# Sharing out the last layer norm of an encoder layer: GpSimd finishes four token tiles, VectorE takes the moments of four

## The reference: what is computed

```
def layer_norm(x, g, b):
    xf = x.astype(jnp.float32)
    mu = xf.mean(-1, keepdims=True)
    var = jnp.square(xf - mu).mean(-1, keepdims=True)
    return ((xf - mu) * lax.rsqrt(var + LN_EPS) * g + b)

x = layer_norm(DEEPNORM_ALPHA * x + moe(x, ...), ln2_g[l], ln2_b[l])
```

## Time and profile before

| what | value |
| --- | --- |
| three timed executions, median | 1329.71 us |
| the profiled execution's own time | 1325.05 us |
| its span, first to last instruction | 1323.2 us |
| busy: PE, DVE, ACT, POOL | 1235.7, 732.8, 590.0, 196.5 us |
| share of the span: PE, DVE, ACT, POOL | 93%, 55%, 45%, 15% |
| chain that ended last, by engine | PE 72%, DMA 7%, DVE 7%, issue 5% |

### The profile page before, as it was taken

The page is one execution under the profiler, slowest core; times in us unless marked ns, Lnnn a source line. Parts: engine busy times, 40 slices in busy tenths (PEclk is TensorE's granted clock), DMA queues, the critical chain, the costliest instruction groups (busy, mean ns, idle before and its releaser), DMA issues.

```text
span 1323.2 us, 21973 instructions
## 1 busy us (share of the span) xinstructions
PE 1235.7 (93%) x8066; PEld 1112.4 (84%) x8066; DVE 732.8 (55%) x1760; ACT 590.0 (45%) x1428; POOL 196.5 (15%) x244
## 2 busy tenths in 40 slices
PE   7999899999999999997799999998899999999993
PEld 6998788888788888886677888897889999999882
DVE  3110355654555455555768876458455565556358
ACT  3221334443444444444543332222365666566455
POOL 0000001200120021011111121001032333233212
PEclk9999999999999999998799999899999999999997
DMA  6534643373437343673354433514889999999773
GB/s 196 158 119 126 161 112 93 81 185 84 108 82 194 79 107 94 159 182 89 98 192 178 152 114 111 223 64 132 306 264 275 265 280 290 272 265 292 188 269 143
DMA packets 157906, 224.35 MB, mean 170 GB/s; under 512 B 40016, under 2 KB 109392, under 8 KB 157776
## 3 DMA queue, kind: packets, MB, share of 16 engines
q1 hardware_dynamic: 146064, 180.28, 45.8%
q0 software_dynamic: 9216, 33.56, 11.1%
q10 hardware_dynamic: 2544, 9.44, 1.8%
HBM read 141.15 MB, written 52.20 MB: 146 GB/s over the span
## 4 chain that ended last, share of the span: by engine, by line
PE 72%; DMA 7%; DVE 7%; issue 5%; SPq 3%; ACT 3%; POOL 1%; DVEq 1%; ACTq 0%; POOLq 0%
PE bank L800 16%; PE bank L802 16%; PE bank L801 16%; PE bank L907 8%; PE bank L794 5%; PE bank L894 4%; PE bank L883 3%; SPq L534 3%; PE bank L884 2%; DMA d_work<-in_w_up 2%; PE bank L1017 2%; DMA acc_scratch<-d_work,dstc 2%; DMA Q<-stage_lo 1%; DVE w_gu_lo L1782 1%; DVE d_work L1980 1%
## 5 line engine op out<-in xcount | busy, mean ns | idle before, releaser
L1262 ACT ACTIVATE b_work<-b_work 128x256 f32<-128x256 f32 (+3 forms) x288 | 148.1, 514 | 267.9 <-DVE b_work L1598 267.1
L800 PE MATMUL bank<-xgT_hi,w_gu_hi 128*128 128x256 f32 x704 | 202.4, 288 | 5.2 <-DVE xgT_lo L1659 2.9
L802 PE MATMUL bank<-xgT_hi,w_gu_lo 128*128 128x256 f32 x704 | 200.4, 285 | 0.0
L801 PE MATMUL bank<-xgT_lo,w_gu_hi 128*128 128x256 f32 x704 | 200.4, 285 | 0.0
L1607 DVE COPY b_work<-bank 128x256 f32<-128x256 f32 (+2 forms) x256 | 112.7, 440 | 118.7 <-PE bank L894 118.2
L800 PEld LDWEIGHTS bank<-xgT_hi,w_gu_hi 128*128 128x128 f32 x704 | 136.3, 194 | 10.7 <-issue 7.5
L2072 POOL CAST Q<-Q 128x512 fp32r<-128x512 f32 x48 | 53.4, 1145 | 595.1 <-DVE w_k_lo L1564 356.0
L801 PEld LDWEIGHTS bank<-xgT_lo,w_gu_hi 128*128 128x128 f32 x704 | 136.3, 194 | 0.1
L802 PEld LDWEIGHTS bank<-xgT_hi,w_gu_lo 128*128 128x128 f32 x704 | 136.2, 194 | 0.0
L894 PE MATMUL bank<-keep,b_work 128*128 128x128 f32 x608 | 117.2, 279 | 16.9 <-ACT b_work L1262 16.9
L894 PEld LDWEIGHTS bank<-keep,b_work 128*128 128x128 f32 x608 | 81.1, 141 | 53.7 <-ACT b_work L1262 23.4
(11 more groups left out here) (192 smaller groups left out, 2820.8 us busy)
## 6 DMA issues: line engine op xcount, KB each, us to landing
d_work<-in_w_gate SPq DMA_DIRECT2D x16, 1024.0 KB, 8.9
d_work<-in_w_up SPq DMA_DIRECT2D x16, 1024.0 KB, 11.4
d_work<-in_w_down SPq DMA_DIRECT2D x16, 1024.0 KB, 10.9
Q<-stage_hi SPq DMA_DIRECT2D x96, 128.0 KB, 2.4
Q<-stage_lo SPq DMA_DIRECT2D x96, 128.0 KB, 2.4
o_scratch<-b_work SPq DMA_DIRECT2D x36, 264.0 KB, 3.2
c_work<-o_scratch SPq DMA_DIRECT2D x12, 792.0 KB, 5.1
raw_w<-in_w_in SPq DMA_DIRECT2D x26, 256.0 KB, 4.2
```

Source lines behind the costliest of these rows:

```text
L800: nc.tensor.matmul(o, w_hi, x_hi, start=first, stop=False)
L801: nc.tensor.matmul(o, w_hi, x_lo, start=False, stop=False)
L802: return nc.tensor.matmul(o, w_lo, x_hi, start=False, stop=last)
L1262: nc.scalar.activation(prob[:, u % 2, 0:n], prob[:, u % 2, 0:n], ACT.Exp, scale=-1.0, bias=o[:, HD:HD + 1], accum_out=o[:, HD + 1:HD + 2])\
```

## The change

Four tiles (0, 1, 2 and 8) are now ended by GpSimd (`final`, six instructions of 512 values for each tile: a `tensor_scalar` that subtracts the mean and multiplies by the root, a multiplication by the gain, an addition of the bias, each in two halves, in place). VectorE ends the other eight. The moments of tiles 3, 4, 11 and 9 are made by VectorE with `bn_stats` and `bn_aggr` (`z_moments`); ScalarE makes the other eight. All results are written in place over the sums (`base`), and the stores go from there, so that `z_out` no longer waits for stores. GpSimd's roots stand in the order 0, 3, 4, 1, 2, 5, 6, 7, 8, 11, 10, 9, with the pieces of `final` between them. SyncE loads the sums of tiles 0, 3, 1 and 4, then the two vectors, then the other eight sums (6, 7, 2, 5, 8, 9, 10, 11); before, the vectors came first, and the sums in the order 0, 1, 6, 7, 2, 3, 8, 9, 4, 5, 10, 11.

```diff
             wait("wg_lo", (more * 2 + 6) * KD)
-            sp.dma_start(ln2g, ln2_g.partition_broadcast(P)).then_inc(S["ln2_loaded"], 16)
-            sp.dma_start(ln2b, ln2_b.partition_broadcast(P)).then_inc(S["ln2_loaded"], 16)
...
-            for t in (0, 1, 6, 7, 2, 3, 8, 9, 4, 5, 10, 11):
+            for t in (0, 3, 1, 4):
+                load_sums(t)
+            sp.dma_start(ln2g, ln2_g.partition_broadcast(P)).then_inc(S["ln2_loaded"], 16)
+            sp.dma_start(ln2b, ln2_b.partition_broadcast(P)).then_inc(S["ln2_loaded"], 16)
+            for t in (6, 7, 2, 5, 8, 9, 10, 11):
+                load_sums(t)
...
+            for t in (3, 0, 4, 5, 6, 1, 2, 7, 11, 10, 9, 8):
+                store(t)
...
                 if n == LATE0 + 1:
-                    for t in range(2):
+                    for t in Z_ACT[0:2]:
                         z_stats(t)
                 if last:
-                    for t in range(2, 5):
+                    for t in Z_ACT[2:6]:
                         z_stats(t)
...
+                if n == LATE0 + 1:
+                    for t in (3, 4):
+                        z_moments(t)
                 if last:
-                    for t in range(1, 5):
-                        z_out(t, t % 2)
+                    for t in (5, 6):
+                        z_out(t)
...
                 h_low(q, s)
+                if n == LATE0 + 1:
+                    z_out(3)
                 if not last and not soon:
                     xg_low(q + 1, 1, n + 1)
                 if n == LATE0 + 1:
-                    z_out(0, 0)
+                    z_out(4)
...
+            def z_moments(t):
+                if t < 2 * EARLY:
+                    dve.wait_ge(S[f"acc_ld{t}"], 16)
+                dve.drain()
+                for c in range(2):
+                    V.bn_stats(zbst[:, c, :], base[:, t, 512 * c:512 * c + 512])
+                dve.drain()
+                V.bn_aggr(zmv[:, t, :], zbst.rearrange("p a b -> p (a b)")).then_inc(S["z_bn"], 1)
...
             add_shared(end - 1, EARLY + LATE - 2, 1)
-            for t in range(5, 7):
-                z_out(t, t % 2)
             for half in range(2):
                 add_shared(end, EARLY + LATE - 1, half)
-            for t in range(7, TILES):
-                z_out(t, t % 2)
+            for t in (11, 9):
+                z_moments(t)
+            for t in (7, 11, 10, 9):
+                z_out(t)
...
+            def final(t, part):
+                n = Z_POOL.index(t)
+                for c in range(2):
+                    w = slice(512 * c, 512 * c + 512)
+                    at = base[:, t, w]
+                    if part == 0:
+                        if c == 0:
+                            pool.wait_ge(S["z_rstd"], Z_ROOTS.index(t) + 1)
+                        end = G.tensor_scalar(at, at, minus_mean[:, t:t + 1], rstd2[:, t:t + 1], ALU.add, ALU.mult)
+                    elif part == 1:
+                        if c == 0:
+                            pool.wait_ge(S["ln2_loaded"], 32)
+                            pool.wait_ge(S["z_part"], 2 * n + 1)
+                        end = G.tensor_tensor(at, at, ln2g[:, w], ALU.mult)
+                    else:
+                        if c == 0:
+                            pool.wait_ge(S["z_part"], 2 * n + 2)
+                        end = G.tensor_tensor(at, at, ln2b[:, w], ALU.add)
+                end.then_inc(S["z_part" if part < 2 else "fin_pool"], 1)
+
+            root(0)
+            final(0, 0)
+            root(3)
+            root(4)
+            final(0, 1)
+            final(0, 2)
+            root(1)
+            final(1, 0)
+            root(2)
+            root(5)
+            final(1, 1)
+            root(6)
+            final(1, 2)
+            root(7)
+            for part in range(2):
+                final(2, part)
+            root(8)
+            final(2, 2)
+            for t in (11, 10, 9):
+                root(t)
+            for part in range(3):
+                final(8, part)
```

More of the change, by code:

```diff
@@ L778, in _, with load_sums, store @@
             acc_t = acc_d.rearrange("(t p) d -> t p d", p=P)
-            for t in (0, 1, 6, 7, 2, 3, 8, 9, 4, 5, 10, 11):
+            def load_sums(t):
                 sp.dma_start(base[:, t, :], acc_t[t]).then_inc(S[f"acc_ld{t}"], 16)
[L781 to L786, removed]
+            for t in (0, 3, 1, 4):
[4 more added lines that the diff above has]
+                load_sums(t)
+            def store(t):
+                if t in Z_POOL:
+                    sp.wait_ge(S["fin_pool"], Z_POOL.index(t) + 1)
+                else:
+                    sp.wait_ge(S["fin_ready"], Z_DVE.index(t) + 1)
+                sp.dma_start(out_t[t], base[:, t, :]).then_inc(S["out_st0"], 16)
+            for t in (3, 0, 4, 5, 6, 1, 2, 7, 11, 10, 9, 8):
+                store(t)
+            sp.wait_ge(S["out_st0"], 16 * TILES)
         @block.tensor
@@ L1534, in _ @@
                 d_step(more * 2 + (EARLY + 4 + n), (n + 1) % 2, LATE0 + n)
-            for t in range(5, TILES):
+            for t in Z_ACT[6:]:
                 z_stats(t)
@@ L1969, in route_done, with z_out @@
                  .then_inc(S["table_ready"], 1)
[L1971 to L1974 removed]
+            def z_moments(t):
[6 more added lines that the diff above has]
+                V.bn_aggr(zmv[:, t, :], zbst.rearrange("p a b -> p (a b)")).then_inc(S["z_bn"], 1)
+            def z_out(t):
+                if t == Z_DVE[0]:
                     dve.wait_ge(S["ln2_loaded"], 32)
[L1976 to L1978 removed]
+                dve.wait_ge(S["z_rstd"], Z_ROOTS.index(t) + 1)
                 dve.drain()
[L1980 removed]
+                if t in Z_BN:
+                    V.scalar_tensor_tensor(zb, base[:, t, :], zmv[:, t, 0:1], ln2g, ALU.subtract, ALU.mult)
+                else:
+                    V.scalar_tensor_tensor(zb, base[:, t, :], minus_mean[:, t:t + 1], ln2g, ALU.add, ALU.mult)
                 dve.drain()
[L1982 removed]
+                V.scalar_tensor_tensor(base[:, t, :], zb, rstd2[:, t:t + 1], ln2b, ALU.mult, ALU.add)\
                  .then_inc(S["fin_ready"], 1)
@@ L2149, in _, with root @@
             add_to_tokens(end)
-            for t in range(TILES):
-                pool.wait_ge(S["z_var"], t + 1)
-                G.tensor_tensor(rstd2[:, t:t + 1], zvar[:, t:t + 1], eps_z, ALU.add).then_inc(S["z_eps"], 1)
-                pool.wait_ge(S["z_eps"], t + 1)
-                G.tensor_tensor(rstd2[:, t:t + 1], rstd2[:, t:t + 1], minus_half, ALU.pow).then_inc(S["z_rstd"], 1)
+            def root(t):
+                n = Z_ROOTS.index(t)
+                if t in Z_ACT:
+                    pool.wait_ge(S["z_var"], Z_ACT.index(t) + 1)
+                else:
+                    pool.wait_ge(S["z_bn"], Z_BN.index(t) + 1)
+                var = zvar[:, t:t + 1] if t in Z_ACT else zmv[:, t, 1:2]
+                G.tensor_tensor(rstd2[:, t:t + 1], var, eps_z, ALU.add).then_inc(S["z_eps"], 1)
+                pool.wait_ge(S["z_eps"], n + 1)
+                G.tensor_tensor(rstd2[:, t:t + 1], rstd2[:, t:t + 1], minus_half, ALU.pow).then_inc(S["z_rstd"], 1)
```

9 lines of the change are left out of this document (7 added, 2 removed).

## The result

The changed kernel is slower, by about as much as forecast. Twenty executions had a median of 1334.51 us, against 1329.62 us for twenty of the kernel before: ratio 1.0034, 95% interval 1.0023 to 1.0045, so +4.5 us (+3.1 to +6.0). Measured again, it was 1334.57 against 1329.42 (medians of 12 and of 35 executions), ratio 1.0040 (1.0026 to 1.0053). One of the 35, at 2000.89 us with a granted clock of 0.555, is left out of the ratio. The prediction was 1336.0 against 1329.71.

What follows compares the result with a forecast made beforehand. VectorE's instruction list was taken as the bound, with TensorE's tail inside it until 1301.8 us. Terms of +3.1, +2.7 and +0.45 summed to +6.3, moving the median from 1329.71 to 1336.0; range 1328.5 to 1342, forecast's own 1333 to 1341.

Steps and rivals of the forecast that it cites:

- the two large terms: Term 1, +3.1 us up to TensorE's end, and Term 2, +2.7 us behind it.
- The turns: GpSimd's wide instructions alternate with VectorE's two-SBUF-input ones, costing VectorE 1.0 us per `tensor_tensor`, 0.85 per `tensor_scalar`.
- Signs: In the changed profile: `scalar_tensor_tensor` mean well above 1.28 us, many 2.1 to 2.3; GpSimd's tail instructions 2.2 to 2.5.
- `tensor_scalar` on GpSimd: 512-value instruction in `final`, priced at 1.15 us from a cast, bounds 0.19 and 2.56; far from 1.15 would be wrong.
- rival 2: GpSimd's `tensor_scalar` is dear: at 2.56 us each, +14.7 us, median 1344.4; at 2.0, 1341; chance 0.11.
- The loads: Sums' loads before step 10 start 1.4 us earlier, but the new order loses 1.3; silu stays at 1269.3, worth 0.
- Term 1: Steps 10 and 11: delayed `xg_low` and `z_out(6)` make TensorE's last products end at 1304.9, not 1301.8: +3.1 us.
- Term 2: Tail behind TensorE: VectorE's remaining list with `final(8)` in turns takes 21.0 us, not 18.3: +2.7 us.
- Term 3: Last stores, tiles 9 and 8: ready together, SyncE issues one behind the other, +0.45 us; landing as before.
- Rival 1: GpSimd's wide work runs beside VectorE's without turns: -4.3 us, median 1325.4; chance 0.14.
- Rival 3: Turns cost half: terms 1 and 2 shrink to +1.5 and 0, sum +2 us, median 1332; chance 0.11.

Runs made afterwards that it cites:

- e7_alldve: The changed kernel with all twelve tiles ended by VectorE, GpSimd making only the roots; ratio 0.9998 to the kernel before, stretch 68.5 us.
- e8_moments: e7_alldve with the moments of tiles 9 and 11 given back to ScalarE; ratio 0.9979 to the kernel before, stretch 65.1 us.
- e3_tile8: The changed kernel with tile 8 ended by VectorE, leaving GpSimd tiles 0, 1 and 2; ratio 1.0026 to the kernel before, stretch 69.4 us.
- e1_narrow: The changed kernel with GpSimd's 512-value instructions cut to one value, four tiles left un-normalised; ratio 0.9979 to the kernel before, stretch 64.3 us.
- e9_early: The changed kernel with the two vectors loaded first again, ahead of the wait for the last additions; ratio 1.0045 to the kernel before, stretch 73.4 us.
- after_again: The changed kernel unedited, measured again for its second profile; ratio 1.0040 to the kernel before, stretch 73.6 us.
- e5_tile0: e4_inplace with tile 0 ended by GpSimd behind its root, vectors still loaded ahead; ratio 0.9971 to the kernel before, stretch 65.9 us.
- e4_inplace: The kernel before with only the results written in place over the sums and stored from there; ratio 0.9996 to the kernel before, stretch 69.5 us.

## Why the prediction was right, and where its steps were wrong

The sum was forecast as +6.3 us, and is +2.6 in the first profile (71.95 - 69.3) and +4.3 in the second; timed +4.5 to +5.2. The time was in the range, and in the forecast's own, and the cause was the one named, but the two large terms were too high. The profile of before has 0.9 us of the lower clock on its path, so that +3.5 is the fairer figure for the first profile. In the changed order this clock wouldn't show, since `z_out(3)` stands ahead of the second half of `xg_low`: `e7_alldve` and `e8_moments` had these transposes at 1.09 and 1.97 us, and both had `gated` of step 11 at +37.9.

- **The turns: right in kind, too dear.** Signs seen as forecast: the 16 instructions' mean rose from 1.286 to 1.837 us; nine are at 2.1 to 2.25. GpSimd's instructions in the tail are at 1.66 and 2.1, below the 2.2 to 2.5 forecast. In the tail a meeting with a `tensor_tensor` costs VectorE 0.83 to 0.85 us (2.12 less 1.285), not 1.0, and one with a `tensor_scalar` 0.34 (1.62 less 1.285), not 0.85. I took the first from a 16-value instruction, which waited 0.93, and the second from a cast. The Trainium skill (SBUF — State Buffer, "SBUF: two separate sides") has the two exclude each other for the whole instruction; by that rule 1.2 us per meeting, and the trace disagrees: 0.83 of GpSimd's 1.26.
- **`tensor_scalar` on GpSimd: wrong.** 0.76 us alone, not 1.15, which the prediction named as a sign against it; rival 2 falls with it. Between its own two values (+6.3 at 1.15, +2.6 at 0.19) 0.76 gives +4.8. The Trainium skill (GPSIMD Engine Reference, "Engine selection") calls one-input work roughly line-rate. From that page's 1.2 GHz ("Specifications") and one value per partition and cycle the estimate is 0.43 us; I had put it at 0.55. The trace's 0.76 agrees with neither, but both are nearer than the cast's 1.15 from which I priced it.
- **The loads: wrong in one place.** They start 1.2 us earlier (2.2 in the second profile), as said. But silu came at +14.7 and +14.4, not at the +15.4 of before: I laid the landings out at the spacing of before, and the second load lands 2.6 us behind the first, not 3.35.
- **Term 1, +3.1: the step that failed.** Measured: -0.1 and +1.6 at TensorE's end. The path is as described: `xg_low` late, `z_out(6)` behind a 0.77 us wait for GpSimd's root. But GpSimd reached that root at +32.4, not +35.9, with silu 0.7 earlier, its `tensor_scalar` instructions short and its meetings cheaper, and `gated` of step 11 was at +38.7, not +41.6. The clock, which I had only as a risk on the slow side, was on the path in the profile of before (1.97 us for the second transposes, 0.9 more than at the higher level) and not after. That is chance and no working of the change, as the transposes above show. In the second profile it fell ahead of step 11 and cost 1.7.
- **Term 2, +2.7: half.** Measured 19.63 - 18.3 = +1.3, the same in both profiles. The layout was right, four meetings with a `tensor_tensor` and two with a `tensor_scalar`, and the prices were not: 4 x 0.83 + 2 x 0.34 = 4.0 us of excess, where I had 5.5. (GpSimd's first two met 1.62 and 1.64, the other four 2.11 to 2.13.)
- **Term 3, +0.45: too small.** The two stores were issued 0.38 us apart, but the second took 3.6 us to land and the first 2.7, where one alone took 2.6: +1.35 in all (4.0 less 2.6). I had priced the issue, not two transfers at once. Where the last store is alone (`e3_tile8`, `e7_alldve`) it lands in 2.6 to 2.7 again.
- **Rivals.** Rival 1 (no turns) is ruled out by the times of 1.6 to 2.25 us, and `e1_narrow`. Its own sum is a little off: -2.1, -2.9 and two issues of 0.45 are -4.1, not -4.3. Rival 3 (half the cost, 1332) is nearest to the first profile's stretch, the forecast (1336.0) to the timed 1334.5. The landing in the middle of the range owes something to errors that cancelled, and that part is luck: terms 1 and 2 too high, term 3 too low, and in the timed runs some 1 to 2 us more than the profiles' stretches have.

The ladder of runs gives each part of the change its own price, by the stretch (by the ratio in brackets): vectors later -3.5 us (-0.0022), of which 0.9 is the clock in the profile of before; in place 0 (-0.0004); tiles 3 and 4's moments and the new orders -0.6 (0.0001); the two moments in the tail +3.35 (+0.0019); GpSimd's four tiles +3.5 to +5.1 (+0.0036 to +0.0042), of which 1.3 is the pair of last stores. Each step is priced on the kernel ahead of it; the vectors' in the changed kernel came out smaller (`e9_early`). So one part of the change was a gain, hidden under two that cost more.

**Open.** For the kernels built from the one before, stretch and ratio agree within 0.7 us. For those built from the changed one the ratio is always worse than the stretch says, by 0.5 us (`e7_alldve`) to 3.4 (`e3_tile8`), 1.0 and 1.9 for the changed kernel itself. 0.3 us of it lies outside the span: the time exceeds the span by 2.2 us in the changed kernel, `e1_narrow`, `e3_tile8`, `e7_alldve` and `e9_early`, and by 1.85 in the others. Ahead of step 10 the profiles show no difference: its `dgu` starts at 1258.6 us in the mean of the seven profiles built from the changed kernel, at 1258.3 in the five others. Where the rest lies, perhaps in a clock that falls more often in the executions that weren't profiled, no run here tells. The prices by stretch and by ratio above are two readings for that reason.

## What to carry to other kernels

Handing part of a busy VectorE's list to an idle GpSimd paid here where the handed work lay beside VectorE's PSUM-reading or idle time, and cost where it lay beside instructions with two SBUF tensors: one tile placed there won 0.2% (0.9971 after 0.9996, 0.9955 after 0.9978), four lost 0.4%. Look first for shorter ends: moments on an engine that is done early, and a load that delays a transfer on the path, both cost or gave some 3 us here without any turn-taking. See that the last two stores don't go out together (1.3 us). Before a difference of 1 us between two profiles is explained, look at the same place in a third: the clock at one standstill moved by as much. And price a new instruction from one of its own kind and width; a 16-value wait and a cast misled me by a fifth and by half.

## What the runs showed of the hardware

- A GpSimd `tensor_scalar` with two column operands on 128x512 float32 takes 0.76 us alone, a `tensor_tensor` 1.26; in turns with VectorE's 1024-value instructions 1.6 to 1.7, and 2.0 to 2.3.
- Two vectors' loads (512 KB each) beside the last indirect additions hold up the sums: their loads start at +4.7 to +5.8 in the four profiles with them, at +3.3 to +4.4 in the eight without.
- A standstill of 3.0 us ahead of the same block was followed by the full clock in one execution (11.8 us) and by the lower level in two others (14.4 and 13.3 us). Ahead of the second transposes, 1.99 us was followed by the lower level (`e8_moments`, 1.97 us for eight) and 1.99, 2.74 and 3.67 by the higher (`after_again`, `e5_tile0`, `e4_inplace`, 1.09). It is a risk with a price, which one profile can't show.
- Two stores of 512 KB issued 0.38 us apart landed 2.7 and 3.6 us after their issue; one alone took 2.6 to 2.7.
